# Weight sums made ahead in device memory for the paired down-projections of a two-block kernel

## The chip, the core and the metric

The kernel runs on one core of a Trainium2 chip. The time is the device time of one execution in microseconds (us), and less is better. The engines in the text: TensorE (PE), VectorE (DVE), ScalarE (ACT), GpSimd (POOL) and SyncE (SP), which here issues the loads of the weights. TensorE's granted clock was at its full level of 2.4 GHz (1.00) in all stretches read here.

## The reference

Two transformer blocks work on 256 rows of 2048 float32 values. The first has attention with compressed, selected and windowed keys (16 heads), a feed-forward of 8192 and a gated projection; the second has sliding-window attention with sinks (32 heads) and a gated feed-forward of 5632 with a short convolution. What matters here are the two down-projections:

```
h = h + y
hn = rms_norm(h, norm_ffn[i])
h = h + jnp.square(jax.nn.relu(hn @ ffn_w1[i])) @ ffn_w2[i]
...
c = conv_w[0] * up[:, 0:S]
for j in range(1, CONV_WIDTH_2):
    c = c + conv_w[j] * up[:, j:j + S]
gate, val = jnp.split(c, 2, axis=-1)
return (jax.nn.silu(gate) * val) @ w_down
```

## The kernel before

**Pieces.** All weights lie in device memory as `wstream`, 757 pieces of 128 x 1024 float32 (512 KB), in the order of use. SP loads one after another into the four slots of `raw` (L557), each as soon as the slot's old piece has its low half (`lo_ready`). ScalarE rounds a piece to its high half `whi` (`split_hi`, L2157), VectorE subtracts that from `raw` for the low half `wlo` (`split_lo`, L1307), and TensorE uses both: a product is three matmuls, high by high, high by low, low by high (`product`, L941 to L943). When TensorE has used a piece it raises `piece_used`, and the halves' slot is free.

**Stages.** Each takes a run of pieces: vs (first piece 0), kv (8), cv (40), misc (56), q (57), wo (89), then ff0, fd0, ff1, fd1, ff2, fd2, proj, ff3, fd3, gate, v2, k2, q2, wo2, and up0, dn0, up1, dn1, up2, dn2. A chunk of 2048 hidden columns is made in an ff or up stage and multiplied down in the fd or dn stage that follows. Every engine runs the same list of pieces by a loop of its own (`body` and `rows_body`), which splits a piece ahead and calls the steps that are due at an index (`between`), so the order of each engine's work is written out by hand. A wait in such a list holds up all that stands behind it on that engine.

**Paired stages.** fd0, fd1, fd2, dn0 and dn1 treat some pairs of pieces as a group (`Pairing`, `down_pair`). A plain pair needs 24 matmuls of 128 x 512: two pieces, two halves of columns, two halves of tokens, three each. A group gets the same from seven products of sums of weights and sums of hidden tiles, so 21. `FIRST` has groups at pairs 3 and 5 of both halves `cp` of the output columns (four a stage, three stages), `SECOND` at 4 and 6 of the first half and 2, 4 and 6 of the second (five a stage, two stages). The four products with sums of weights go to banks of their own (`side_bank`, ONE, FIVE, SEVEN, SIX) or to a main bank.

The weight sums are made in the stage: VectorE (in dn0 and dn1 POOL, but for the first group) adds halves of the two raw pieces (`t_first`: L1777 and L1779, on POOL L2736 and L2738), VectorE adds twice more (`t_second`: L1785, L1787), ScalarE rounds the four sums (`t_highs`, L2418, L2420) and VectorE subtracts for the low halves (`t_lows`, L1794):

```
V.tensor_tensor(sums_at(c)[:, 0, :], raw[:, x % SLOTS, 0:WIDE], raw[:, x % SLOTS, WIDE:], ALU.add)
V.tensor_tensor(sums_at(c)[:, 1, :], raw[:, x % SLOTS, WIDE:], raw[:, y % SLOTS, WIDE:], ALU.add)
V.tensor_tensor(sums_at(c)[:, 2, :], sums_at(c)[:, 0, :], y[:, WIDE:], ALU.add)
V.tensor_tensor(sums_at(c)[:, 3, :], sums_at(c)[:, 2, :], y[:, 0:WIDE], ALU.add)
```

At the end of a half's last group VectorE takes the side banks into the result (`sides_in`, five operations, L1807 to L1819, after ScalarE's `copy_side`), later the main banks (`mains_in`); TensorE's second half waits for the first of these. The sums of hidden tiles (`mix`, `mix_high`, `mix_low`) and the corrections (`corners`) are POOL's and ScalarE's.

**Around it.** In ff0 to ff3 ScalarE applies the rectifier and the square (`relu_squared`, L2373) one piece after TensorE has finished a tile, to `zr`, which POOL has made (`take`, L2661). In the q and q2 stages POOL scales the attention's probabilities (`nsa_scale`, L2691, and `swa_scale`) for TensorE's turns (L753 in q). ScalarE issues the load of `xrows` (2 MiB) in kv and six moves of V at the start of q (L2329 to L2338). POOL issues no transfer.

Of the kernel before, what the change touches and what calls it, by code (L numbers as in the profile page):

```python
# [26 lines left out]
P = 128  # L27
S = 256
# [36 lines left out]

STAGES = [("vs", 2, 16), ("kv", 16, 16), ("cv", 4, 32), ("misc", 3, 2), ("q", 16, 16), ("wo", 8, 16)]
# [12 lines left out]
_p = _u = _z = 0  # L79
for _name, _n, _k in STAGES:  # L80
    PB[_name], UB[_name], ZB[_name] = _p, _u, _z
# [95 lines left out]
class Pairing:  # L177


    def __init__(self, fast, sides, mains, last_sides):  # L180
        self.fast, self.sides, self.mains, self.last_sides = fast, sides, mains, last_sides
        self.mixed = sorted({m for ms in fast for m in ms})
        self.groups = [(cp, n, m) for cp, ms in enumerate(fast) for n, m in enumerate(ms)]
        self.x_at = {16 * cp + 2 * m: g for g, (cp, n, m) in enumerate(self.groups)}
        self.at_x = {g: x for x, g in self.x_at.items()}

    def used(self, cp):
        return len(self.fast[0]) + (len(self.fast[1]) if cp else 0)


FIRST = Pairing(((3, 5), (3, 5)), sides=12, mains=17, last_sides=28)
SECOND = Pairing(((4, 6), (2, 4, 6)), sides=14, mains=16, last_sides=32)
DN = FF_CHUNKS - 1


# [32 lines left out]
def program(nc, xT, pT, wstream, consts, setup, params, grows, xrows, out):  # L228
# [9 lines left out]
    bias_rows = nc.dram_tensor("bias_rows", [SWA_HEADS, RB], F32)  # L238

    with ExitStack() as ctx:  # L240
# [15 lines left out]
        with nc.sbuf_tensor("Tboth", [P, 2, 4, WIDE], FR) as Tboth:  # L256
            pass
        y = sb("y", [P, DT, S])

        with nc.sbuf_tensor("Tlow", [P, 4, WIDE], FR) as Tlow:  # L260
            pass
# [33 lines left out]
        def ring(flat, a, n=4, w=S):  # L295
# [4 lines left out]
        Tsum = ptf.rearrange("p (n c) -> p n c", n=4)  # L300
        Tcopy = [Tboth[:, h, :, :] for h in range(2)]
        tCf = tC.rearrange("p n w -> p (n w)")
        corner, cross = tCf[:, 0:WIDE], tCf[:, WIDE:2 * WIDE]
        mixsum = kT[:, :, :, :].rearrange("p a g c -> p (a g c)")[:, 0:3 * WIDE].rearrange("p (n i q) -> p n i q", n=3, i=4)
        mixed = [vT[:, 0:3, :].rearrange("p n (i q) -> p n i q", i=4),
                 mixlo[:, 4 * S:4 * S + 3 * WIDE].rearrange("p (n i q) -> p n i q", n=3, i=4)]
        Tsum2 = bflat[:, 4 * S:4 * S + 4 * WIDE].rearrange("p (n c) -> p n c", n=4)
        Tcopy2 = [vT[:, :, :], Tlow[:, :, :]]
        mixsum2 = bflat[:, 4 * S + WIDE:4 * S + 4 * WIDE].rearrange("p (n i q) -> p n i q", n=3, i=4)
        mixhi2 = mixhi[:, 0:3 * WIDE].rearrange("p (n i q) -> p n i q", n=3, i=4)  # L310
        mixlo2 = [pA[:, n, :, :].rearrange("p h (i q) -> p (h i) q", i=2) for n in range(2)]
        mixlo2.append(PTr.rearrange("p a b -> p (a b)")[:, 4 * (S + 4):4 * (S + 4) + 2 * S].rearrange("p (i q) -> p i q", i=4))
# [88 lines left out]
        t_sum, t_more, t_hi = Again(c_taken, 5 * KVG), Again(cpad_zero, 1), Again(c_exp, KVG)  # L401
        t_lo, t_used = Again(c_shift, KVG), Again(c_scores, KVG)
# [6 lines left out]
        x_scaled = sem("x_scaled")  # L409
# [29 lines left out]

        def sums_at(c):  # L440

            return Tsum2 if is_down2(c) else Tsum

        def sums_part(c, h):

            return (Tcopy2 if is_down2(c) else Tcopy)[h]
# [19 lines left out]
        def pairing(c):  # L466

            return SECOND if is_down2(c) else FIRST

# [73 lines left out]
        def _(sp):  # L543
# [11 lines left out]
            def load(i, s):  # L555
                sp.wait_ge(lo_ready, i - SLOTS + 1)
                sp.dma_start(raw[:, s, :], wstream[ds(i, 1)].rearrange("a p n -> p (a n)")).then_inc(raw_landed[s], 16)  # L557

            with sp.Fori(1, NPIECE // SLOTS - 1) as it:
                for j in range(SLOTS):  # L560
                    load(it * SLOTS + (SLOTS + j), j)
            for i in range(NPIECE // SLOTS * SLOTS, NPIECE):
                sp.wait_ge(lo_ready, i - SLOTS + 1)
                sp.dma_start(raw[:, i % SLOTS, :], wstream[i]).then_inc(raw_landed[i % SLOTS], 16)
            for t in range(QT):
                for f in range(4):

                    sp.wait_ge(fin_out, 4 * t + f + 1)
                    w = slice(f * WIDE, f * WIDE + WIDE)
                    sp.dma_start(out[:, t, w], xN[:, t, w]).then_inc(out_done, 16)  # L570
# [4 lines left out]
        def _(pe):  # L575
# [358 lines left out]
            def hidden(c, it, **more):  # L934
                ff, _, o = chunk_at(c)
                units(o * 64 + it * 8 + PB[ff], PB[ff], o * 24 + it * 4 + UB[ff], UB[ff], 4, DT,
# [8 lines left out]
            def down_pair(c, cp):  # L945

                _, fd, o = stage_at(c)
                p, z0 = o * 64 + (PB[fd] + 16 * cp), o * 24 + (4 + UB[fd])
                early, late = slice(0, P), slice(P, 2 * P)

                def weights(i, f):

                    s, w = (PB[fd] + 16 * cp + i) % SLOTS, slice(f * WIDE, f * WIDE + WIDE)
                    return whi[:, s, w], wlo[:, s, w]

                def hidden(i, tok):

                    return H[:, i, 0, tok], H[:, i, 1, tok]

                def mix_of(m, i):  # L960

                    return tuple(mixed_at(c, pairing(c).mixed.index(m), h)[:, i, :] for h in range(2))

                def sums(i):

                    return sums_part(c, 0)[:, i, :], sums_part(c, 1)[:, i, :]

                def arrive(i):

                    pe.wait_ge(lo_ready, p + (i + 1))  # L970
                    if cp == 0 and is_down2(c):
                        pe.wait_ge(up_ready, (c - DN) * CH + i + 1)
                    elif cp == 0:
                        pe.wait_ge(ff_ready, c * CH + (i + 1))

                def plain(i, f):

                    for t in range(QT):
                        last = product(main_bank(c, cp, 2 * f + t), *hidden(i, slice(t * P, t * P + P)), *weights(i, f), i == 0, i == 15)
                    return last  # L980

                def group(i, g):

                    _, n, m = pairing(c).groups[g]
                    lone, final = n == 0, n == len(pairing(c).fast[cp]) - 1
# [1958 lines left out]
```

## Time and profile before

| what | us |
|---|---|
| median of 3 runs | 2193.86 (2193.68 to 2193.93) |
| profiled execution, its own time | 2195.73 |
| its span | 2193.9 |
| TensorE busy | 2180.1 (99%) |
| VectorE busy | 1566.5 (71%) |
| ScalarE busy | 1133.5 (52%) |
| POOL busy | 711.8 (32%) |

Busy shares are averages over stages with different limits. Matmuls are pipelined: the time of one in a row is longer than the distance between two starts. A timeline row gives the start, the duration, and in brackets how long the engine had been idle and what released it; "x3" joins three of the same kind. In a window row the counts in brackets are instructions; then come TensorE's granted clock, the busy share of the 16 DMA engines and what they moved.

### The profile page before, as it was taken

Reading aid. Unit: us, or ns where it says so; the run is one execution under the profiler, and the core shown is the slowest. Engines: PE = TensorE matmul, PEld = TensorE weight load, DVE = VectorE, ACT = ScalarE, POOL = GpSimd, SP = SyncE. Lnnn points to the kernel's source line nnn. Section 1 sums busy time; section 2 is a strip of 40 time slices with the busy share of each in tenths; the row PEclk is TensorE's granted clock in tenths of the full one; section 3 lists DMA queues with packets and bytes.
Section 4 is the critical chain, followed back from the end, with each engine's and each line's share of the span. In section 5 each row is a group of like instructions: output and inputs, shape, how many; then the busy total and the mean of one; then the engine's idle time right before and its main releaser. Section 6 shows DMA issues by size and latency. Waiting matters only on the chain.

```text
span 2193.9 us, 34076 instructions
## 1 busy us (share of the span) xinstructions
PE 2180.1 (99%) x11511; PEld 1862.4 (85%) x11511; DVE 1566.5 (71%) x2187; ACT 1133.5 (52%) x1720; POOL 711.8 (32%) x625
## 2 busy tenths in 40 slices
PE   9999999999999999999999999999999999999998
PEld 7888988888888888888888887788888888888887
DVE  6876767558657757755878667567778777787775
ACT  6445555545445545454556455465455455554553
POOL 3202320361362263153000033005554355533531
PEclk9999999999999999999999999999999999999999
DMA  7665335556556556566565654545555665555664
GB/s 250 231 224 171 116 130 181 174 184 211 191 182 209 192 184 207 202 194 197 177 199 188 225 171 137 192 163 182 189 195 185 202 198 192 188 191 197 200 207 149
DMA packets 118084, 414.35 MB, mean 189 GB/s; under 512 B 12896, under 2 KB 18048, under 8 KB 117472
## 3 DMA queue, kind: packets, MB, share of 16 engines
q1 hardware_dynamic: 111600, 401.37, 55.7%
q10 hardware_dynamic: 6384, 11.70, 1.7%
q8 instruction: 57, 0.93, 0.2%
q14 instruction: 43, 0.35, 0.0%
HBM read 409.29 MB, written 2.15 MB: 188 GB/s over the span
## 4 chain that ended last, share of the span: by engine, by line
PE 93%; DVE 4%; ACT 1%; DMA 1%; POOL 1%; issue 1%; SPq 0%; DVEq 0%; ACTq 0%; POOLq 0%
PE bank L607 33%; PE bank L615 17%; PE bank L941 6%; PE bank L943 6%; PE bank L942 6%; PE bank L664 2%; PE bank L666 2%; PE bank L665 2%; DVE wboth L1307 2%; PE bank L1269 1%; PE bank L1267 1%; PE bank L1268 1%; PE bank L740 1%; PE bank L1202 1%; PE bank L777 1%; PE bank L917 1%
## 5 line engine op out<-in xcount | busy, mean ns | idle before, releaser
L1307 DVE TENSOR_TENSOR wboth<-raw,wboth 128x1024 fp32r<-128x1024 f32 (+1 forms) x756 | 953.8, 1267 | 468.1 <-ACT wboth L2157 459.8
L2157 ACT CAST wboth<-raw 128x1024 fp32r<-128x1024 f32 (+1 forms) x756 | 773.0, 1034 | 469.3 <-PE bank L943 123.3
L607 PE MATMUL bank<-A,wboth 128*128 128x512 f32 x2928 | 705.4, 392 | 0.5 <-DVE wboth L1307 0.3
L607 PEld LDWEIGHTS bank<-A,wboth 128*128 128x128 f32 x2928 | 536.8, 188 | 105.3 <-issue 1.3
L615 PEld LDWEIGHTS bank<-A,wboth 128*128 128x128 f32 x2928 | 376.7, 191 | 14.8
L615 PE MATMUL bank<-A,wboth 128*128 128x256 f32 x2928 | 384.0, 283 | 0.0
L941 PE MATMUL bank<-wboth,H 128*128 128x512 f32 x508 | 197.8, 389 | 1.2 <-DVE wboth L1307 1.2
L943 PE MATMUL bank<-wboth,H 128*128 128x512 f32 x508 | 197.6, 389 | 0.0
L942 PE MATMUL bank<-wboth,H 128*128 128x512 f32 x508 | 197.6, 389 | 0.0
L2661 POOL TENSOR_TENSOR PT<-z,rs 128x256 f32<-128x256 f32 x88 | 92.5, 1052 | 263.4 <-DVE z L1338 261.3
L2661 POOL TENSOR_TENSOR bias<-z,rs 128x256 f32<-128x256 f32 x64 | 104.7, 1635 | 197.9 <-DVE z L1338 109.4
L1338 DVE TENSOR_REDUCE z<-bank 128x256 f32<-128x512 f32 x172 | 117.6, 685 | 12.2 <-PE bank L607 12.1
L2373 ACT ACTIVATE Sm<-bias 128x256 f32<-128x256 f32 x64 | 26.7, 418 | 171.2 <-POOL bias L2661 171.2
L941 PEld LDWEIGHTS bank<-wboth,H 128*128 128x128 f32 x508 | 95.4, 188 | 21.8 <-DVE wboth L1307 2.0
L943 PEld LDWEIGHTS bank<-wboth,H 128*128 128x128 f32 x508 | 95.4, 188 | 19.8
L942 PEld LDWEIGHTS bank<-wboth,H 128*128 128x128 f32 x508 | 95.4, 188 | 19.7
L2766 POOL TENSOR_TENSOR x<-x,Sm 128x512 f32<-128x512 f32 x18 | 35.4, 1995 | 206.8 <-DVE x L1841 137.6
L2611 ACT ACTIVATE PT<-PT,par 128x256 f32<-128x256 f32 x88 | 44.8, 509 | 98.0 <-POOL PT L2661 98.0
L2661 POOL TENSOR_TENSOR kT<-z,rs 128x256 f32 (+1 forms) x12 | 11.3, 946 | 248.8 <-DVE z L1338 248.8
L2077 DVE SCALAR_TENSOR_TENSOR Sm<-PT,par 128x256 f32<-128x256 f32 x88 | 50.4, 573 | 51.7 <-ACT PT L2611 51.7
L2805 POOL TENSOR_TENSOR bias<-Sm 128x256 f32<-128x256 f32 x44 | 72.4, 1645 | 39.6 <-DVE Sm L2080 39.3
L607 PE MATMUL bank<-H,wboth 128*128 128x512 f32 x320 | 79.1, 394 | 0.0
(387 smaller groups left out, 3160.7 us busy)
## 6 DMA issues: line engine op xcount, KB each, us to landing
raw<-wstream SPq DMA_DIRECT2D x756, 512.0 KB, 3.4
bias<-bias_rows ACTq DMA_DIRECT2D x6, 512.0 KB, 5.4
x<-xrows ACTq DMA_DIRECT2D x1, 2048.0 KB, 9.1
bias<-grows ACTq DMA_DIRECT2D x2, 1024.0 KB, 6.4
out<-x SPq DMA_DIRECT2D x8, 256.0 KB, 2.1
x<-xT SPq DMA_DIRECT2D x7, 256.0 KB, 5.3
pA<-bias_rows ACTq DMA_DIRECT2D x2, 512.0 KB, 6.9
Sm<-grows ACTq DMA_DIRECT2D x1, 1024.0 KB, 6.6
```

The lines of the kernel that those rows point to most:

```text
L607: last = nc.tensor.matmul(bank(j)[:, :], whi[:, s, cols(i)], moving(j, k), start=(k == 0), stop=(k == K - 1))
L615: last = nc.tensor.matmul(bank(j)[:, 0:S], wlo[:, s, cols(i)], moving(j, k)[:, 0, :], start=False, stop=False)
L941: nc.tensor.matmul(bank[:, :], a_hi, w_hi, start=start, stop=False)
L942: nc.tensor.matmul(bank[:, :], a_hi, w_lo, start=False, stop=False)
L943: return nc.tensor.matmul(bank[:, :], a_lo, w_hi, start=False, stop=stop)
L1307: V.tensor_tensor(wlo[:, s, 0:w], raw[:, s, 0:w], whi[:, s, 0:w].bitcast(F32), ALU.subtract).then_inc(lo_ready, 1)
L1338: V.tensor_reduce(dst(j) if dst else z[:, (z0 + j) % 4, :], bank[:, :].rearrange("p (h c) -> p c h", h=2), AX, ALU.add).then_inc(z_ready, 1)
L2077: V.scalar_tensor_tensor(tA[:, slot, :], ub[:, slot, 1:S + 1], w[1], c0[:, slot % 2, :], ALU.mult, ALU.add).then_inc(up_step, 1)
L2157: C.copy(whi[:, s, 0:w], raw[:, s, 0:w]).then_inc(hi_ready, 1)
L2611: C.activation(c0[:, j % 2, :], ub[:, j % 4, 0:S], ACT.Copy, scale=par[:, ds(PO["conv"][0] + 3 * (2 * t0 + j), 1)]).then_inc(up_c0, 1)
L2661: return lambda zz: G.tensor_tensor(dst, zz, by, ALU.mult)
L2805: G.tensor_tensor(zr[:, slot + 1, :], tC[:, slot, :], tB[:, slot + 1, :], ALU.mult).then_inc(up_h, 1)
```

## The change

A tensor `weight_sums` in device memory takes, for each of now 24 groups, two pieces of 512 KB with the four sums.

- SP issues 24 plain copies of 1 MiB within device memory (both raw pieces of a group), twelve after the loads of pieces 11, 15, ... 55 (kv and cv), twelve from piece gate + 3 on, every fourth piece, which ends in v2.
- POOL issues transfers that add in device memory: for each group one of 512 KB and one of 256 KB (`sum_first`), then one of 512 KB (`sum_last`). Those of fd0 and fd1 and the first part of fd2's go out in q, fd2's last ones in wo; those of dn0 and dn1 in q2, dn1's last ones in wo2.
- In the paired stages a group is now four entries of the list: piece w + 1 (512 KB), the first half of piece w (256 KB), and the two pieces of sums (512 KB each, loaded by SP into `y` or `kT`, and then cast and subtracted like any piece: `sum_hi`, `sum_lo`). The order of products in a group is main 0, main 2, ONE, FIVE, SEVEN, SIX, main 1. `t_first`, `t_second`, `t_highs` and `t_lows` are gone on all engines.
- `SECOND` has six groups, at pairs 2, 4 and 6 of both halves. The mixed hidden tiles get other buffers. `sides_in` and `copy_side` stand four entries behind the beginning of a half's last group.
- ScalarE's `relu_squared` comes two pieces behind TensorE instead of one (`each_lag=2`).
- SP's and POOL's loops are written out with fixed addresses, and some semaphores are used again.

```diff
+FIRST = Pairing(((3, 5), (3, 5)))
+SECOND = Pairing(((2, 4, 6), (2, 4, 6)))
...
+            def load_pairs(c):
...
+                    if m in at.fast[cp]:
+                        g = at.used(0) * cp + at.fast[cp].index(m)
+                        load(PB[fd] + i, wstream[w + 1], past[0])
+                        load(PB[fd] + i + 1, wstream[w, :, 0:WIDE], past[1])
+                        if g == 0:
+                            sp.wait_ge(sums_done, 16 * group_of(c + 1, 0))
...
+                        for h in range(2):
+                            load_sum(c, i + 2 + h, g, h)
...
+            def sum_copy(c, g):
+
+                if c and g == 0:
+                    sp.wait_ge(sums_copied, 16 * group_of(c, 0))
+                x, n = first_weight(c, g), group_of(c, g)
+                sp.dma_start(weight_sums[2 * n:2 * n + 2], wstream[x:x + 2]).then_inc(sums_copied, 16)
...
+            copy_at = {**{PB["kv"] + 3 + 4 * i: at for i, at in enumerate(early)}, **{PB["gate"] + 3 + 4 * i: at for i, at in enumerate(late)}}
...
-                    product(side_bank(c, cp, ONE), *hidden(i, early), *weights(i, 0), lone, final).then_inc(piece_used, 1)
+                    arrive(i, 2 * m + 1)
+                    product(main_bank(c, cp, 0), *hidden(2 * m + 1, early), *weights(i, 0))
+                    pe.wait_ge(*mix_ready.at(mix_count(c, at.mixed.index(m) + 1)))
+                    product(main_bank(c, cp, 2), *mix_of(m, 3), *weights(i, 1)).then_inc(piece_used, 1)
                     arrive(i + 1)
-                    product(main_bank(c, cp, 0), *hidden(i + 1, early), *weights(i + 1, 0))
-                    pe.wait_ge(*mix_ready.at(mix_count(c, pairing(c).mixed.index(m) + 1)))
-                    product(main_bank(c, cp, 2), *mix_of(m, 3), *weights(i + 1, 1)).then_inc(piece_used, 1)
-                    pe.wait_ge(*t_lo.at(2 * group_of(c, g) + 1))
-                    product(side_bank(c, cp, FIVE), *mix_of(m, 1), *sums(0), lone, final)
-                    product(side_bank(c, cp, SEVEN), *mix_of(m, 0), *sums(1), lone, final)
-                    pe.wait_ge(*t_lo.at(2 * group_of(c, g) + 2))
-                    product(side_bank(c, cp, SIX), *mix_of(m, 2), *sums(2), lone, final)
-                    product(main_bank(c, cp, 1), *hidden(i + 1, late), *sums(3)).then_inc(t_used.sem, 1)
+                    product(side_bank(c, cp, ONE), *hidden(2 * m, early), *weights(i + 1, 0), lone, final).then_inc(piece_used, 1)
+                    arrive(i + 2)
+                    product(side_bank(c, cp, FIVE), *mix_of(m, 1), *weights(i + 2, 0), lone, final)
+                    product(side_bank(c, cp, SEVEN), *mix_of(m, 0), *weights(i + 2, 1), lone, final).then_inc(piece_used, 1)
+                    arrive(i + 3)
+                    product(side_bank(c, cp, SIX), *mix_of(m, 2), *weights(i + 3, 1), lone, final).then_inc(t_used.sem, 1)
+                    product(main_bank(c, cp, 1), *hidden(2 * m + 1, late), *weights(i + 3, 0)).then_inc(piece_used, 1)
...
-                steps_of.update({at.sides: lambda: sides_in(c, 0), at.mains: lambda: mains_in(c, 0, range(4)), at.last_sides: lambda: sides_in(c, 1),
-                                 30: lambda: mains_in(c, 1, range(2)), 31: lambda: mains_in(c, 1, range(2, 4))})
-                rows_body(p, PB[fd], 32, 1, lambda f: None, steps_of, 0, ahead, at.x_at)
+                steps_of = {at.over[0]: lambda: sides_in(c, 0), at.middle + (0 if is_down2(c) else 1): lambda: mains_in(c, 0, range(4)),
+                            at.count if is_down2(c) else at.over[1]: lambda: sides_in(c, 1),
+                            at.count - 2: lambda: mains_in(c, 1, range(2)), at.count - 1: lambda: mains_in(c, 1, range(2, 4))}
+                rows_body(o * CHP + PB[fd], PB[fd], at.count, 1, lambda f: None, steps_of, halves=at.halves, c=c)
...
-                body(o * 64 + it * 8 + PB[ff], PB[ff], o * 8 + it, 4, DT, relu_squared, **more)
+                body(o * CHP + it * 8 + PB[ff], PB[ff], it, 4, DT, relu_squared, each_lag=2, laps=o * CHUNK_LAPS, **more)
...
+            def sum_first(c, i):
+
+                g = i // 2
+                x, n = first_weight(c, g), group_of(c, g)
+                pool.wait_ge(sums_copied, 16 * group_of(c + 1, 0))
+                if i % 2:
+                    pool.dma_start(weight_sums[2 * n + 1, :, 0:WIDE], wstream[x + 1, :, WIDE:], accum_op=ALU.add).then_inc(sums_half, 16)
+                else:
+                    pool.dma_start(weight_sums[2 * n].rearrange("p (f w) -> p f w", f=2), wstream[x:x + 2, :, WIDE:].rearrange("a p w -> p a w"),
+                                   accum_op=ALU.add).then_inc(sums_half, 16)
...
+                pool.dma_start(weight_sums[2 * n + 1].rearrange("p (f w) -> p f w", f=2),
+                               weight_sums[2 * n, :, 0:WIDE].unsqueeze(1).to_broadcast([P, 2, WIDE]), accum_op=ALU.add).then_inc(sums_done, 16)
...
+                sums_early(i)
+            for g in range(len(FIRST.groups)):
+                pool.wait_ge(piece_used, SLOTS + PB["wo"] + 22 + 2 * g)
+                sum_last(2, g)
```

## Rows read from the trace of the kernel before

**Rows 1.** part 1 of the page: busy time of each engine, share of the span, instructions

```profile
PE 2180.1 (99%) x11511; PEld 1862.4 (85%) x11511; DVE 1566.5 (71%) x2187; ACT 1133.5 (52%) x1720; POOL 711.8 (32%) x625
```

**Rows 2.** waits of TensorE: line waited for, us in total, times, longest

```profile
PE bank L941 <- DVE wboth L1307: 1.2, 1, 1.2
```

**Rows 3.** windows: fd0, stretch of plain pieces; PE, PEld, DVE, ACT, POOL, clock, DMA, GB/s

```profile
520.30:531.18 10.88, 10.88 (x49) 9.01 (x49) 7.33 (x7) 4.21 (x4) 5.70 (x3) 1.00 0.67 230
```

**Rows 4.** timeline of TensorE in fd0 (start, us): the gap

```profile
501.39 0.39 PE L943 MATMUL bank<-wboth,H 128*128 128x512 f32 x1
502.95 0.50 PE L941 MATMUL bank<-wboth,H 128*128 128x512 f32 x1 [1.17 <-DVE wboth L1307]
```

**Rows 5.** timeline of VectorE at that gap

```profile
497.45 1.77 DVE L1777 TENSOR_TENSOR PT<-raw 128x512 f32<-128x512 f32 x1
...
501.06 0.69 DVE L1787 TENSOR_TENSOR PT<-PT,raw 128x512 f32<-128x512 f32 x1
501.67 1.22 DVE L1307 TENSOR_TENSOR wboth<-raw,wboth 128x1024 fp32r<-128x1024 f32 x1
```

**Rows 6.** all waits: ScalarE's before the rectifier

```profile
ACT Sm L2373 <- POOL bias L2661: 171.2, 64, 3.4
```

**Rows 7.** timeline of VectorE in dn0, sides at the turn

```profile
1678.24 0.69 DVE L1807 COPY y<-bank 128x512 f32<-128x512 f32 x1 [0.19 <-PE bank L943]
...
1680.76 0.69 DVE L1819 TENSOR_TENSOR Sm<-Sm,bank 128x512 f32<-128x512 f32 x1
```

**Rows 8.** timeline of TensorE there, first matmul after the group

```profile
1678.04 0.39 PE L941 MATMUL bank<-wboth,H 128*128 128x512 f32 x1
```

**Rows 9.** tile raw: durations min/median/max in ns of cast and subtract

```profile
L2157 ACT CAST wboth<-raw x756: 611/1048/1069, 9.5 to 2175.3; 128x1024 fp32r<-128x1024 f32 x179, 128x512 fp32r<-128x512 f32 x10
L1307 DVE TENSOR_TENSOR wboth<-raw,wboth x756: 676/1225/2596, 10.6 to 2176.4; 128x1024 fp32r<-128x1024 f32 x179, 128x512 fp32r<-128x512 f32 x10
```

**Rows 10.** windows: two of kv, two of cv, two of q, one of gate and v2

```profile
60.00:70.00 10.00, 10.00 (x57) 8.74 (x56) 7.88 (x11) 3.20 (x4) 0.74 (x1) 1.00 1.00 395
70.00:80.00 10.00, 10.00 (x57) 8.74 (x56) 8.89 (x9) 5.80 (x5) 3.12 (x2) 1.00 0.43 140
134.10:141.50 7.40, 7.40 (x41) 6.39 (x40) 3.93 (x5) 3.80 (x4) 0.00 (x0) 1.00 0.85 268
141.50:148.90 7.40, 7.40 (x41) 6.39 (x40) 4.90 (x4) 4.60 (x5) 0.00 (x0) 1.00 0.81 287
165.00:180.00 15.00, 15.00 (x83) 13.08 (x82) 8.68 (x16) 6.87 (x8) 2.21 (x3) 1.00 0.95 266
177.00:290.00 113.00, 113.00 (x709) 101.47 (x708) 82.57 (x242) 63.93 (x159) 34.22 (x37) 1.00 0.39 126
1080.00:1220.00 140.00, 139.76 (x633) 115.55 (x631) 112.28 (x176) 80.66 (x127) 0.00 (x0) 1.00 0.58 189
```

**Rows 11.** DMA issues: KB each, median us from issue to landing

```profile
x<-xrows ACTq DMA_DIRECT2D x1, 2048.0 KB, 9.1
```

**Rows 12.** timeline of TensorE in cv and at its end

```profile
137.81 1.11 PE L851 MATMUL bank<-wboth,H 128*120 128x256 f32 x8
...
145.21 1.11 PE L851 MATMUL bank<-wboth,H 128*120 128x256 f32 x8
...
152.97 0.42 PE L873 MATMUL bank<-A,wboth 128*48 128x512 f32 x1
```

**Rows 13.** timeline of VectorE in cv

```profile
131.75 2.36 DVE L1307 TENSOR_TENSOR wboth<-raw,wboth 128x1024 fp32r<-128x1024 f32 x2 [1.15 <-ACT wboth L2157]
...
141.94 3.73 DVE L1307 TENSOR_TENSOR wboth<-raw,wboth 128x1024 fp32r<-128x1024 f32 x3 [1.57 <-ACT wboth L2157]
...
148.95 2.52 DVE L1307 TENSOR_TENSOR wboth<-raw,wboth 128x1024 fp32r<-128x1024 f32 x2 [1.18 <-ACT wboth L2157]
```

**Rows 14.** timeline of POOL in q

```profile
186.42 2.96 POOL L2691 TENSOR_TENSOR Sm<-Sm,small 128x512 f32<-128x512 f32 x2
```

**Rows 15.** timeline of TensorE in q

```profile
191.43 0.82 PE L753 MATMUL bank<-con,Sm 128*128 128x128 f32 x6
```

More of the change, by code:

```diff
@@ L63, with __init__, used @@
 PW = BLK * P
+class Pairing:
+    def __init__(self, fast):
+        self.fast = fast
+        self.mixed = sorted({m for ms in fast for m in ms})
+        self.groups = [(cp, n, m) for cp, ms in enumerate(fast) for n, m in enumerate(ms)]
+        self.begin, at = {}, 0
+        for cp in range(2):
+            for m in range(8):
+                self.begin[cp, m] = at
+                at += 4 if m in fast[cp] else 2
+        self.middle, self.count = self.begin[1, 0], at
+        self.halves = {self.begin[cp, m] + 1 for cp, _, m in self.groups}
+        self.over = [self.begin[cp, fast[cp][-1]] + 4 for cp in range(2)]
+    def used(self, cp):
+        return len(self.fast[0]) + (len(self.fast[1]) if cp else 0)
+DN = FF_CHUNKS - 1
+FIRST = Pairing(((3, 5), (3, 5)))
+SECOND = Pairing(((2, 4, 6), (2, 4, 6)))
+PAIRED = {**{f"fd{c}": FIRST for c in range(DN)}, "dn0": SECOND, "dn1": SECOND}
+NGROUP = sum(len(at.groups) for at in PAIRED.values())
+CHP = 64 + 2 * len(FIRST.groups)
 STAGES = [("vs", 2, 16), ("kv", 16, 16), ("cv", 4, 32), ("misc", 3, 2), ("q", 16, 16), ("wo", 8, 16)]
@@ L553, in _, with load @@
             sp.dma_start(con[:, :], consts).then_inc(in_k, 16)
[L555 to L564, printed above, removed]
+            def load(i, src, past=SLOTS):
+                s = i % SLOTS
+                sp.wait_ge(lo_ready, i - past + 1)
+                sp.dma_start(raw[:, s, 0:src.shape[-1]], src).then_inc(raw_landed[s], 16)
@@ L960, in mix_of, with arrive @@
                 def mix_of(m, i):
[L962 to L968, printed above, removed]
+                    return tuple(mixed_at(c, at.mixed.index(m), h)[:, i, :] for h in range(2))
+                def arrive(i, k=None):
                     pe.wait_ge(lo_ready, p + (i + 1))
[L971 to L974, printed above, removed]
@@ L976, in plain @@
-                def plain(i, f):
+                    if cp == 0 and k is not None and is_down2(c):
+                        pe.wait_ge(up_ready, (c - DN) * CH + k + 1)
+                    elif cp == 0 and k is not None:
+                        pe.wait_ge(ff_ready, c * CH + (k + 1))
+                def plain(i, k, f):
                     for t in range(QT):
-                        last = product(main_bank(c, cp, 2 * f + t), *hidden(i, slice(t * P, t * P + P)), *weights(i, f), i == 0, i == 15)
+                        last = product(main_bank(c, cp, 2 * f + t), *hidden(k, slice(t * P, t * P + P)), *weights(i, f), k == 0, k == 15)
@@ L2128, in _ @@
                 if t == 0:
-                    dve.wait_ge(dn_half, 1)
+                    dve.wait_ge(*dn_half.at(1))
                 else:
@@ L2787, in _ @@
             pool.wait_ge(acc_zero, 1)
+            for g in range(len(SECOND.groups)):
+                pool.wait_ge(piece_used, SLOTS + PB["wo2"] + 16 + 2 * g)
+                sum_last(DN + 1, g)
             pool.wait_ge(rs_ready, 6)
```

322 lines of the change are left out of this document (166 added, 156 removed).

## The prediction

> **What bounds the kernel now.** I read the profile's first part, then TensorE's waits, and last the queues in the few places that the change touches. TensorE is busy for 2180.1 us, 99% of a span of 2193.9 us [rows 1]. Its waits are short and few; the one that this change can reach is a single 1.2 us at L941 for VectorE's L1307 [rows 2]. So time is won by fewer matmuls or by that wait, and lost wherever something new is late for TensorE. The pace is not the 389 ns of a row, which is a latency: in the paired stage fd0 49 matmuls start within 10.88 us [rows 3], and four plain pieces are 48, so one matmul of 128x512 costs 10.88/48 = 0.227 us.
>
> The sums below are made against the profiled execution, 2195.73 us, of which 2193.9 us are its span. The median of the runs is 2193.86 us, 1.87 us lower; I take the same difference off the median. 0.2% is 4.4 us, about what a measurement of this kernel can tell from no change: the lines lie at 2189.5 and 2198.2 us.
>
> **1. Fewer products.** The second pairing goes from five groups to six, in dn0 and in dn1. A group stands for a plain pair of pieces: 21 matmuls for 24. Two groups more are 6 matmuls: 6 x 0.227 = **-1.4 us**, all of it on TensorE's path.
>
> **2. The stall in fd0.** From the matmul at 501.39 to the next at 502.95 pass 1.56 us in place of 0.23 [rows 4]: 1.3 us lost; with a slow start behind it I take 1.4. VectorE explains it: between 497.45 and 501.75 it makes four additions of weights (L1777, L1779, L1785, L1787) with only one half-piece subtract among them, and the whole-piece subtract L1307 on which TensorE waits starts at 501.67 [rows 5]. All these additions leave the stage, so the subtract moves up by most of these 4.3 us; the copies now made for the sums are 3.5 pieces a group at 1.05 us on ScalarE and 1.22 us on VectorE [rows 9], 3.7 and 4.3 us against the group's 21 x 0.227 = 4.8 us of TensorE. Both fit. **-1.4 us.** No such wait stands in the other paired stages, so the additions taken out there give nothing; neither do the POOL additions of dn0 and dn1.
>
> **3. Rectifier and square a piece later.** ScalarE stood 171.2 us before L2373 for POOL, at most 3.4 us at a time [rows 6]. Behind that wait stand the casts of the next pieces. A piece later the wait is mostly over when it is asked for, and casts come earlier. TensorE, however, has no idle time in ff0 to ff2, so this is cover for step 2 and worth 0 itself. H is ready one piece later; the last tiles of H are read in the stage after, by its last pieces, and the first ones were made in the first quarter of the ff stage: 0.
>
> **4. The turn in dn0 and dn1 between the two halves of the columns.** Before, VectorE begins the five additions of the sides at 1678.24 us and ends at 1680.76 + 0.69 = 1681.45 [rows 7]. TensorE, from the matmul at 1678.04, has one plain pair to do before it needs those banks: 24 x 0.227 = 5.45 us, up to 1683.49 [rows 8]; 2.0 us were spare. After, the sides stand in the list behind the low half of the piece after next, whose slot the group's end frees: a cast of 1.05 and a subtract of 1.22 us [rows 9] go first. 2.3 + 3.2 = 5.5 us, with an assumed 0.15 us between the engines 5.65 us against 5.45: 0.2 us late, twice: **+0.4 us**. Both ends: 0 if the slot frees a product earlier, 1 us each if the cast waits behind another. In fd0 to fd2 two plain pairs, 10.9 us, lie there: nothing.
>
> **5. Copies in SP's queue.** SP issues 24 copies of 1 MiB from device memory to device memory among the loads of the weights, each in front of the next load. No row shows such a copy. Lower bound: the densest loads, 395 GB/s at a DMA share of 1.00 [rows 10], 1.049 MB in 2.65 us. Upper bound: read and written each at that price, 5.3 us. Between them lies the nearest row, the load of xrows: 2 MiB in 9.1 us from issue to landing, beside the weights' loads [rows 11], so 4.55 us a MiB. I take c = 4.5 us; both ends stay for the range.
>
> Where do they hurt? The twelve late ones fall in 1080 to 1220 us, where the engines are in use for 0.58 of the time [rows 10]; one copy comes with four pieces, and four pieces last 48 x 0.227 = 10.9 us, of which 0.42 x 10.9 = 4.6 us are free: c fits, 0. Eight early ones fall in kv: beside the load of xrows the share is 1.00, in the ten us behind it 0.43 [rows 10], so 10.9 us have some 6 us free for one copy: 0, with the copy beside xrows as the tightest. Four fall in cv, behind pieces 43, 47, 51 and 55. There four pieces go in 145.21 - 137.81 = 7.40 us [rows 12], which is 2.10 MB, 283 GB/s, and the DMA share is 0.85 and 0.81 [rows 10]: this stage is close to its loads. In such a cycle, which has one copy, the engines have 0.15 x 7.4 = 1.1 us free around copy 47 and 0.19 x 7.4 = 1.4 us around 51 and, I assume, 55. Then there is the lead of the low half over TensorE: 131.75 + 2.36 = 134.11 against 137.81, 3.7 us behind copy 47; 141.94 + 1.23 = 143.17 against 145.21, 2.0 us behind copy 51; 148.95 + 1.26 = 150.2 against 152.97, 2.8 us behind copy 55 [rows 12, 13]. Copy 43 has no smaller lead than 47. Each stall is c less the free time less the lead: at c = 4.5, 0 + 1.1 + 0.3 = **+1.4 us**; at 2.65, 0; at 5.3, 0.5 + 1.9 + 1.1 = 3.5; at 7, 2.2 + 3.6 + 2.8 = 8.6.
>
> The Trainium skill (DMA: Bandwidth & Descriptors, section Latency and other measured facts) states 207 to 214 GB/s in each direction for copies between tensors of device memory; by it, as an estimate, c would be 5.0 us and the whole sum 1.2 us higher than mine. No row here shows it.
>
> **6. POOL's accumulating transfers.** POOL issues 36 in q and wo and 36 later, on a queue of its own, for 1.25 MiB a group. It issues none before. In q the DMA share is 0.39 [rows 10]. Two places can feel it: the moves of V among the same engines, with a share of 0.95 in 165 to 180 us [rows 10], and POOL's own scaling: L2691 ends at 189.38 us and TensorE's turn L753 reads it at 191.43 [rows 14, 15], 2.05 us later, so an issue of under 2 us between them costs nothing. Lower end 0, upper end some 3 us (one late turn a whole scaling, 2.96 us [rows 14]). I take **+0.5 us**, near the lower end, since 2 us is the smallest slack that I found. The Trainium skill (DMA: Bandwidth & Descriptors, section Issuing engines are not separate DMA queues) says that such transfers share the 16 engines with the loads whatever queue issues them; it speaks against the change in the way already priced here.
>
> **7. More to load in the paired stages.** A group loads 1.75 MiB instead of 1. In dn a group and its plain pair are 45 x 0.227 = 10.2 us for 2.75 MiB, 2.88 MB: 282 GB/s. That is cv's rate, which runs there without a stall, and 395 GB/s were reached elsewhere: 0, covered by 2.9 us of spare DMA time in each such period; without that cover the rival C.
>
> **Sum.** -1.4 - 1.4 + 0.4 + 1.4 + 0.5 = -0.5 us: 2195.2 for a profiled execution, **2193.4 us** for the median.
>
> **Rivals.**
> A, slower: the copies hold up the loads in cv. Mechanism as in 5, place 134 to 153 us, price 3c - 12.4 us once all three stalls are open. Without it the sum is -1.9 us, so it takes 6.3 us of stall, c above 6.2 us (under 170 GB/s), to be slower by 0.2%; at c = 7 the time is 2193.86 - 1.9 + 8.6 = 2200.6 us. For it: the share of 0.81 to 0.85, and that a copy reads and writes the same memory. Against it: the upper bound from rows, 5.3 us, lies below 6.2, unless a copy's write is dearer than its read. Chance 0.22.
> B, all hidden: c near 2.65 us, and nothing from POOL. -1.4 - 1.4 + 0.4 = -2.4: 2191.5 us, still within 0.2%. For it: copies of large rows are the densest form of transfer, and TensorE stands nowhere in cv now. Chance 0.27.
> C, the sums arrive late: loads in dn fall to the 268 GB/s of cv's thinner stretch [rows 10], 2.88 MB in 10.75 us in place of 10.2, 12 periods: +6.5 us, 2199.7 us. Against it: cv's rate is what its pieces asked for. Chance 0.04.
> D, faster by over 0.2%: it would take 1.6 us more than steps 1 and 2 and no cost at all; no row offers that. Also, the change might not do what it says (sums that are waited for in full): that is C. Chance 0.05.
>
> **Numbers.** My forecast itself has 0.42 (c from about 3.5 to 6). Faster 0.05 (D), same 0.69 (forecast and B), slower 0.26 (A and C). The range reaches from B with step 4 at its lower end, 2191.0, to A at c = 7, 2200.6; outside are D, the far end of A and part of C, under 0.2.
>
> **What would show it.** TensorE's matmuls fall by 6; the interval of 1.56 us at fd0's first group is gone; in cv TensorE has one or two gaps of about a microsecond, released by the subtract to the low half, behind a wait of ScalarE for a load; the DMA share there nears 1; a gap of 0.2 us at the turns of dn0 and dn1. Wrong if: TensorE stands still in q or q2 behind POOL; if gaps appear inside groups (late sums); or if cv's gaps add up to more than 6 us.

## The result and the profile after

The changed kernel takes 2203.05 us (median of 5 runs, 2200.2 to 2205.89) against 2193.86 us (5 runs, 2193.45 to 2194.59): 9.2 us slower, ratio 1.0043 with a 95% interval of 1.0031 to 1.0054. That is above the range of the prediction. The times also scatter over 5.7 us, where those of the kernel before lie within 1.1 us (3.6 us over the 28 runs of a later set). The profiled execution of the changed kernel took 2201.86 us, with a span of 2200.0 us.

The page of the changed kernel: TensorE's busy time and instructions, then two DMA queues (packets, MB, share of 16 engines).

```profile
PE 2180.7 (99%) x11505; PEld 1863.1 (85%) x11505; DVE 1548.6 (70%) x2119; ACT 1146.8 (52%) x1724; POOL 731.9 (33%) x681
...
q1 hardware_dynamic: 119280, 445.41, 59.0%
q0 software_dynamic: 16512, 31.46, 8.5%
```

The six matmuls are gone (11505 in place of 11511 [rows 1]), and still the span is longer. q0 is new: POOL's adding transfers. They hold the engines for 0.085 x 2200 = 187 us for 31.46 MB, 168 GB/s. The loads and SP's plain copies, in q1, move 445.41 MB in 0.590 x 2200 = 1298 us, 343 GB/s. By the time of its packets, a byte added takes twice as long as a byte of q1.

TensorE's waits in the changed kernel (line waited for, us, times, longest), the three longest:

```profile
PE bank L817 <- POOL y L2706: 3.3, 1, 3.3
PE bank L854 <- DVE PTr L1590: 2.1, 1, 2.1
PE bank L938 <- DVE bias L1701: 2.1, 1, 2.1
```

The wait of [rows 2] is not among them; these three are new. Where they lie is told best by the same matmul, counted from the first, in the two timelines:

| place | before, us | after, us | after less before | lost here |
|---|---|---|---|---|
| start of kv | 44.29 | 41.93 | -2.4 | |
| end of cv | 152.60 | 152.75 | 0.15 | 2.5 |
| q, behind the first long wait | 189.81 | 196.45 | 6.6 | 6.5 |
| q, behind the second | 280.14 | 289.14 | 9.0 | 2.4 |
| fd0, first group | 502.95 | 510.41 | 7.5 | -1.5 |
| first matmuls ahead of up0 | 1458.77 | 1465.76 | 7.0 | -0.5: 0.2 close behind the row above, 0.3 here |
| dn0, the turn | 1683.03 | 1690.34 | 7.3 | 0.3 |
| dn2 | 2185.70 | 2191.79 | 6.1 | -1.2: six matmuls -1.4, dn1's turn 0.3 |

The first line is no work of the change: the first 44 us differ from the kernel before by -2.4 to 1.2 us in the profiled executions below, and between kernels that do the same there (1.2 in five, -2.1 in seven). From there on the change lost 8.5 us net: 11.4 us in cv and q and 0.6 at the turns, against some 3.4 us won.

**The wait of 3.3 us at 187 us.** The DMA issues (KB each, median us from issue to landing) of the changed kernel:

```profile
weight_sums<-wstream POOLq DMA_DIRECT2D x24, 512.0 KB, 9.4
weight_sums<-weight_sums POOLq DMA_DIRECT2D x24, 512.0 KB, 8.9
...
H<-H ACTq DMA_DIRECT2D x1, 256.0 KB, 13.2
vT<-PT ACTq DMA_DIRECT2D x1, 256.0 KB, 6.2
H<-PT ACTq DMA_DIRECT2D x1, 256.0 KB, 9.7
```

The same two moves of `H` in the DMA issues of the kernel before:

```profile
H<-H ACTq DMA_DIRECT2D x1, 256.0 KB, 6.9
H<-PT ACTq DMA_DIRECT2D x1, 256.0 KB, 6.6
```

Then ScalarE's timeline there in the changed kernel, and a row of POOL's with two of TensorE's; the brackets give the idle time ahead.

```profile
174.62 1.05 ACT L2202 CAST wboth<-raw 128x1024 fp32r<-128x1024 f32 x1 [1.72 <-PE bank L692]
182.84 0.47 ACTq L2392 DMA_DIRECT2D vT<-PT  x1
...
184.06 1.05 ACT L2202 CAST wboth<-raw 128x1024 fp32r<-128x1024 f32 x1 [8.40 <-issue]
...
193.05 1.99 ACT L2202 CAST wboth<-raw 128x1024 fp32r<-128x1024 f32 x2 [5.02 <-DMA H<-PT]
```

```profile
189.97 0.72 POOL L2706 TENSOR_TENSOR y<-z,bias 128x256 f32<-128x256 f32 x1 [9.26 <-DVE z L1782]
...
186.33 1.11 PE L692 MATMUL bank<-A,wboth 128*128 128x256 f32 x8
190.74 1.22 PE L817 MATMUL bank<-kT,y 128*128 128x256 f32 x2 [3.30 <-POOL y L2706]
```

The two last moves of `H` landed 13.2 and 9.7 us after issue, in place of 6.9 and 6.6 us. ScalarE waits for the first before it issues the next pair, and for the second before it goes on: the first is issued at 169.59 and lands 13.2 us later, at 182.8, where the next issue stands. So it stood 8.4 us and then 5.0, and its casts stand behind those waits. VectorE's subtract, its reduction for `y`, POOL's scaling of `y` and TensorE's scores follow in a chain; POOL had been idle for 9.26 us when the reduction released it. And the wait has a sequel. Windows of the changed kernel (columns as in [rows 3]):

```profile
190.00:195.00 5.00, 4.26 (x12) 3.54 (x13) 1.58 (x2) 1.95 (x2) 4.55 (x5) 0.50 1.06 304
195.00:200.00 5.00, 5.00 (x27) 4.38 (x27) 4.17 (x13) 3.08 (x12) 0.88 (x2) 0.84 1.00 233
```

TensorE's granted clock is 0.50, 1.2 GHz in place of 2.4, for the matmuls behind the wait; the mean of 0.84 in the second window puts its end at 196.6 us, 5.9 us behind the wait's end. Counted matmul by matmul, of the 6.5 us 0.2 lie ahead of the wait, 3.5 are the wait and 2.8 the slow matmuls.

**The wait of 2.1 us at 287 us.** POOL, VectorE, ScalarE and TensorE in their timelines of the changed kernel:

```profile
279.92 1.04 POOL L2756 DMA_DIRECT2D weight_sums<-weight_sums  x1 [6.92 <-DMA weight_sums<-weight_sums]
280.50 2.52 POOL L2736 TENSOR_TENSOR Sm<-Sm,small 128x512 f32<-128x512 f32 x2
...
280.59 2.47 DVE L1573 TENSOR_SCALAR small<-small 128x8 f32<-128x8 f32 x1
...
283.09 0.40 ACT L2278 ACTIVATE Sm<-Sm,small 128x128 f32<-128x128 f32 x1 [3.88 <-DVE small L1573]
...
289.14 0.50 PE L854 MATMUL bank<-PTr,vT 128*128 128x256 f32 x2 [2.10 <-DVE PTr L1590]
```

POOL stood 6.92 us in its list for a transfer that it had issued itself at 271.93: the first last addition of fd1 waits until those of fd0 have landed. The scaling queued behind, L2736, was so late that it began 0.09 us ahead of VectorE's L1573. That operation on 8 columns, 0.17 us in the kernel before (L1493 at 273.86), took 2.47 us and ended with POOL's. ScalarE's exponentials, VectorE's `PTr` and TensorE came 2 us later. The Trainium skill (SBUF — State Buffer, section Who interferes with whom) says that VectorE, in the two-port modes that an operation of this kind can enter, and GpSimd share a port pair, which the one that issues first holds for its whole instruction while the other stands. That VectorE stood for POOL this trace bears out: the two ends, 280.59 + 2.47 and 280.50 + 2.52, agree within 0.04 us. It stood for two instructions of POOL (x2), though, and who was first does not decide it in run one below.

**The wait of 2.1 us at the end of cv.** ScalarE, VectorE and TensorE in their timelines of the changed kernel:

```profile
150.06 1.05 ACT L2202 CAST wboth<-raw 128x1024 fp32r<-128x1024 f32 x1 [1.27 <-DMA raw<-wstream]
...
151.14 1.23 DVE L1381 TENSOR_TENSOR wboth<-raw,wboth 128x1024 fp32r<-128x1024 f32 x1 [1.09 <-ACT wboth L2202]
152.28 0.42 DVE L1701 TENSOR_REDUCE bias<-bank 120x128 f32<-120x256 f32 x1
...
150.28 0.39 PE L799 MATMUL bank<-wboth,A 128*128 128x512 f32 x1
152.75 0.66 PE L938 MATMUL bank<-con,bias 120*128 120x60 f32 x4 [2.08 <-DVE bias L1701]
```

This is the chain of step 5: a load behind a copy, a cast, a subtract. TensorE does not wait for the subtract itself but for the reduction that stands behind it in VectorE's list. In the kernel before, this reduction ended 0.8 us ahead of the matmul that needs it:

```profile
151.39 0.42 DVE L1621 TENSOR_REDUCE bias<-bank 120x128 f32<-120x256 f32 x1
...
152.60 0.55 PE L861 MATMUL bank<-con,bias 120*128 120x60 f32 x4
```

### The profile page after: what moved, and what is told of

It is laid out like the page before. It is cut to its first block, busy times and chain, and to the rows that moved or that the text cites. A ratio compares the mean times of both kernels' runs of the same rounds, so it can differ in the third digit from the quotient of the medians.

```text
span 2200.0 us, 31525 instructions
## 1 busy us (share of the span) xinstructions
PE 2180.7 (99%) x11505; PEld 1863.1 (85%) x11505; DVE 1548.6 (70%) x2119; ACT 1146.8 (52%) x1724; POOL 731.9 (33%) x681
## 3 DMA queue, kind: packets, MB, share of 16 engines
q1 hardware_dynamic: 119280, 445.41, 59.0%
q0 software_dynamic: 16512, 31.46, 8.5%
## 4 chain that ended last, share of the span: by engine, by line
PE 92%; DVE 5%; ACT 1%; DMA 1%; issue 1%; DVEq 0%; POOL 0%; ACTq 0%
PE bank L684 33%; PE bank L692 17%; PE bank L1018 6%; PE bank L1019 6%; PE bank L1020 6%; PE bank L741 2%; PE bank L743 2%; PE bank L742 2%; DVE wboth L1381 2%; PE bank L817 1%; PE bank L1341 1%; PE bank L1342 1%; PE bank L1343 1%; DMA raw<-wstream 1%; PE bank L854 1%; PE bank L1276 1%
## 5 line engine op out<-in xcount | busy, mean ns | idle before, releaser
L1381 DVE TENSOR_TENSOR wboth<-raw,wboth 128x1024 fp32r<-128x1024 f32 x756 | 962.0, 1283 | 382.6 <-ACT wboth L2202 378.0
L2202 ACT CAST wboth<-raw 128x1024 fp32r<-128x1024 f32 x756 | 778.9, 1035 | 588.5 <-PE bank L692 162.4
L1018 PE MATMUL bank<-wboth,H 128*128 128x512 f32 x520 | 202.7, 390 | 0.3
L1019 PE MATMUL bank<-wboth,H 128*128 128x512 f32 x520 | 202.5, 389 | 0.0
L1020 PE MATMUL bank<-wboth,H 128*128 128x512 f32 x520 | 202.5, 389 | 0.0
L2795 POOL TENSOR_TENSOR Sm<-Sm 128x256 f32<-128x256 f32 x64 | 81.1, 1267 | 136.0 <-ACT Sm L2428 136.0
L1018 PEld LDWEIGHTS bank<-wboth,H 128*128 128x128 f32 x520 | 97.6, 188 | 21.4 <-DVE Sm L1864 1.1
L1020 PEld LDWEIGHTS bank<-wboth,H 128*128 128x128 f32 x520 | 97.7, 188 | 20.3
L1019 PEld LDWEIGHTS bank<-wboth,H 128*128 128x128 f32 x520 | 97.6, 188 | 20.1
L2706 POOL TENSOR_TENSOR kT<-z,rs 128x256 f32 (+1 forms) x12 | 12.3, 1029 | 246.1 <-DVE z L1412 246.1
L741 PE MATMUL bank<-wboth,H 128*128 128x512 f32 x192 | 75.0, 390 | 0.0
```

The lines of the kernel that those rows point to most:

```text
L741: nc.tensor.matmul(bank[:, :], src[:, k, 0, tok], whi[:, s, w], start=(k == 0), stop=False)
L1018: nc.tensor.matmul(bank[:, :], a_hi, w_hi, start=start, stop=False)
L1019: nc.tensor.matmul(bank[:, :], a_hi, w_lo, start=False, stop=False)
L1020: return nc.tensor.matmul(bank[:, :], a_lo, w_hi, start=False, stop=stop)
L1381: V.tensor_tensor(wlo[:, s, 0:w], raw[:, s, 0:w], whi[:, s, 0:w].bitcast(F32), ALU.subtract).then_inc(lo_ready, 1)
L2202: C.copy(whi[:, s, 0:w], raw[:, s, 0:w]).then_inc(hi_ready, 1)
```

## Experiments

The theory after the comparison: the adding transfers of POOL take DMA time from the moves of V (`vT` and `H` in the rows above), POOL's wait for its own transfers costs the second stall, and the copies cost the one in cv. The rivals stand in the expectations.

**One: the first adding transfers behind the moves of V.**

```diff
-                if 1 <= i < 4 * n + 1:
-                    sum_first(*divmod(i - 1, 2 * n))
+                if 2 * n + 1 <= i < 4 * n + 1:
+                    for j in range(2):
+                        sum_first(*divmod(2 * (i - 2 * n - 1) + j, 2 * n))
```

> The first sixteen adding transfers of q (fd0 and fd1) go out at pieces 9 to 16 of q, two a piece, instead of one at each of pieces 1 to 16: none while the moves of V are under way. Theory T (the adding transfers share the DMA engines with the moves of V, ScalarE stands for these moves, 8.4 and 5.0 us in the changed kernel, and the chain over VectorE and POOL reaches TensorE at 187 us): the 6.5 us lost between 187 and 195 us go, down to 0 to 1; the stall at 287 us stays; about 2196.5 us in place of 2203.0. Rival R1 (it is the loads of weights, catching up after the copies in cv, that slow the moves): nothing changes in q, 2203. Rival R2 (POOL's time for the issues, 1.0 to 1.3 us each, makes its own work late): with two issues a piece the stalls grow, over 2203.

Measured: 2196.02 us (2194.12 before in the same set). The DMA issues of this kernel:

```profile
H<-H ACTq DMA_DIRECT2D x1, 256.0 KB, 6.2
vT<-PT ACTq DMA_DIRECT2D x1, 256.0 KB, 4.1
H<-PT ACTq DMA_DIRECT2D x1, 256.0 KB, 6.1
```

The moves land as before the change, and the first wait is gone, with the copies in cv still there: R1 falls. R2 falls too, since POOL now issues two transfers a piece and no new stall comes, and since in the changed kernel POOL stood idle for VectorE at this place. The Trainium skill (DMA: Bandwidth & Descriptors, section Issuing engines are not separate DMA queues) has the rule of step 6, that transfers share the 16 engines whatever queue issues them; that ScalarE's moves land in 6.2 and 6.1 us once POOL's transfers are out of their way, in place of 13.2 and 9.7, agrees with it.

The second stall stays, 2.2 us of waiting. VectorE and POOL here:

```profile
275.07 2.71 DVE L1573 TENSOR_SCALAR small<-small 128x8 f32<-128x8 f32 x1
...
275.21 2.52 POOL L2736 TENSOR_TENSOR Sm<-Sm,small 128x512 f32<-128x512 f32 x2
```

VectorE's operation begins 0.14 us ahead of POOL's scaling (0.32 us ahead in run three) and still ends with it. POOL's issue of a transfer, from 274.64, was under way by then. What held VectorE from its start, the issue or the scaling, no run shows.

This wait also has a sequel that the changed kernel's has not. The window behind it, and the one behind the equally long wait (2.2 us) of run three:

```profile
283.80:287.10 3.30, 3.25 (x15) 3.23 (x16) 2.61 (x5) 0.99 (x2) 2.31 (x3) 0.50 1.09 179
```

```profile
289.80:293.10 3.30, 3.30 (x25) 3.17 (x26) 2.71 (x6) 1.71 (x3) 2.38 (x3) 1.00 1.07 166
```

In one the granted clock was 0.50 and the stall cost 1.5 us more; in three it was 1.00. What decides it, the runs do not show.

**Two: fd1's last additions in wo.**

```diff
-                elif 5 * n + 2 <= i < 7 * n + 2:
+                elif 5 * n + 2 <= i < 6 * n + 2:
...
-            for g in range(len(FIRST.groups)):
-                pool.wait_ge(piece_used, SLOTS + PB["wo"] + 22 + 2 * g)
-                sum_last(2, g)
+            for c, first in ((1, 6), (2, 22)):
+                for g in range(len(FIRST.groups)):
+                    pool.wait_ge(piece_used, SLOTS + PB["wo"] + first + 2 * g)
+                    sum_last(c, g)
```

> The last four adding transfers of fd1 go out in wo instead of at pieces 26 to 29 of q, so that POOL does not wait in q for those of fd0 to land (6.9 us at 273 us). Theory T: POOL's scaling is then not late, it does not fall on VectorE's small operation (2.47 us in place of 0.17), and the 2.4 us at 287 us go: about 2200.6 us in place of 2203.0; the stall at 187 us stays. A rival, that the operation of VectorE and with it the stall come from the DMA traffic of these transfers as such: the traffic of fd0's four stays, so 1 us or more of the stall stays, 2202 or more.

Measured: 2199.42 us. VectorE and POOL in this kernel's timelines:

```profile
279.88 0.17 DVE L1573 TENSOR_SCALAR small<-small 128x8 f32<-128x8 f32 x1
...
274.74 2.04 POOL L2736 TENSOR_TENSOR Sm<-Sm,small 128x512 f32<-128x512 f32 x2 [2.44 <-DVE small L1582]
```

POOL's scaling is five us ahead of VectorE's operation, which takes 0.17 us again, and TensorE's wait at L854 is gone, so the rival falls; the stall at 187 us stays. In the three profiles in which POOL's wait makes the scaling fall on this operation (the changed kernel, this run's neighbours one and three) it took 2.47, 2.71 and 2.88 us.

**Three: fd2's copies in q.**

```diff
-            copy_at = {**{PB["kv"] + 3 + 4 * i: at for i, at in enumerate(early)}, ...
+            copy_at = {**{PB["kv"] + 3 + 4 * i if i < 8 else PB["q"] + 17 + 4 * (i - 8): at for i, at in enumerate(early)}, ...
```

> The four copies of 1 MiB for fd2 go out behind pieces 17, 21, 25 and 29 of q instead of behind four pieces of cv. Theory T: the gaps of 0.3 and 2.2 us in cv go, the 6.5 us at 187 us stay: about 2200.5 us in place of 2203.0. Rival R1: without the copies nothing has to catch up at the beginning of q, the moves of V land in time and both stalls go, 2194.

Measured: 2200.29 us. TensorE's longest waits in this kernel:

```profile
PE bank L817 <- POOL y L2706: 4.7, 1, 4.7
PE bank L854 <- DVE PTr L1590: 2.2, 1, 2.2
```

The wait at L938 is gone and both in q stay, the first with 7.6 us lost in place of 6.5: R1 falls a second time.

**Four: no adding transfers.** The diff takes out the three transfers of POOL with their waits; SP waits for the copies in place of the sums.

> No adding transfers at all, so the paired stages multiply with the raw copies in place of the sums; the plain copies and all else stay. Theory T: both stalls in q go (6.5 and 2.4 us), the one in cv (2.5 us) and those of the turns (0.4 us twice) stay: 2194 us. Rival R1: only the 2.4 us at 287 us go, 2200.6. Rival R2 gives 2194 like T; the first run of this set tells those two apart.

Measured: 2194.20 us, 8.9 us under the changed kernel, whose median is from another set (the kernel before: 2193.86 there, 2194.12 here). Both stalls of q are gone from TensorE's waits, the one in cv is 1.5 us in this profile. So the adding transfers, beside the moves of V and by POOL's wait for them, are the whole of what was lost in q.

**Five and six: everything moved, with and without an earlier turn.** Five has the three diffs above and this one; six has only the three.

```diff
-                steps_of = {at.over[0]: lambda: sides_in(c, 0), ...
+                steps_of = {at.over[0] - (1 if is_down2(c) else 0): lambda: sides_in(c, 0), ...
...
-                steps_of.update({at.over[0]: lambda: copy_side(c, 0), ...
+                steps_of.update({at.over[0] - (1 if is_down2(c) else 0): lambda: copy_side(c, 0), ...
```

> The three moves of the first set together (adding transfers behind the moves of V, fd1's last ones in wo, fd2's copies in q), and in dn0 and dn1 the sides are taken in one entry earlier at the turn, ahead of the low half that waits for the group's end. Theory T: all that the change cost is gone (6.5, 2.4, 2.5 us and 0.4 us twice) and what it gained stays, 1.4 us for six matmuls and 1.5 us in fd0: about 2191 us, 2.9 us under the kernel before. Rival: moved transfers collide at their new places and take back what was won, 2194 us or more.

> As the run with all four, but the sides at the turn stay where the change put them. Theory T: 0.4 us more in each of dn0 and dn1, 0.8 us over that run, about 2192; in the trace two waits of 0.3 us at the turns, which the other has not. Rival: the cast that stands ahead is no matter, both kernels show the same waits and the same time.

Measured: 2190.99 and 2191.44 us, against 2194.64 us before in this set: ratios 0.9983 (0.9974 to 0.9992) and 0.9984 (0.9975 to 0.9993). Both beat both kernels. Between the two the difference of the medians, 0.45 us, is within the scatter; the traces tell them apart. TensorE's timeline at the turn of dn0 without the earlier sides, then with them:

```profile
1680.44 0.39 PE L1020 MATMUL bank<-wboth,H 128*128 128x512 f32 x1
1680.97 0.50 PE L1018 MATMUL bank<-wboth,H 128*128 128x512 f32 x1
```

```profile
1681.59 0.39 PE L1020 MATMUL bank<-wboth,H 128*128 128x512 f32 x1
1681.81 0.39 PE L1018 MATMUL bank<-wboth,H 128*128 128x512 f32 x1
```

0.53 us from start to start without, 0.22 with; the matmul behind the gap is slower too, by 0.1 us. dn1 shows the same. From 44 us to the last matmuls the kernel without takes 0.9 us longer.

**Seven and eight: what took the stall in fd0 away?** Seven sets `each_lag=1` in the kernel of five; eight is the kernel before with `each_lag=2` alone:

```diff
-                    for step, behind in ((late, lag), (each, 1)):
+                    for step, behind in ((late, lag), (each, each_lag)):
...
-                body(o * 64 + it * 8 + PB[ff], PB[ff], o * 8 + it, 4, DT, relu_squared, **more)
+                body(o * 64 + it * 8 + PB[ff], PB[ff], o * 8 + it, 4, DT, relu_squared, each_lag=2, **more)
```

> As the run with all four, but ScalarE's rectifier and square stand one piece behind TensorE again, as before the change. Theory T: the stall in fd0 went because VectorE's additions left the stage, so it stays away: the same time, about 2191. Rival: it went because ScalarE's casts no longer wait for POOL; then 1.2 to 1.5 us come back at fd0's first group, about 2192.4.

> The kernel before, with only ScalarE's rectifier and square a piece later in ff0 to ff3. Theory T: VectorE's four additions still stand ahead of the subtract that TensorE waits for, so the wait in fd0 stays, 0.8 us or more of 1.5: 2193 to 2194. Rival: with earlier casts VectorE comes to its additions earlier and the wait goes: about 2192.5.

Measured: 2190.81 us for seven, the same as five. For eight 2192.94 us, 1.7 us under the kernel before in its set, but with an interval that reaches no change (ratio 0.9991, 0.9981 to 1.0); the trace decides, and my theory fell there. VectorE's timeline of eight:

```profile
491.90 1.77 DVE L1777 TENSOR_TENSOR PT<-raw 128x512 f32<-128x512 f32 x1
...
496.12 1.22 DVE L1307 TENSOR_TENSOR wboth<-raw,wboth 128x1024 fp32r<-128x1024 f32 x1
```

The same additions stand ahead of the same subtract and take the same time, but all of it is 5.5 us earlier than in [rows 5], and the first matmul of that piece starts at 500.12 with no wait. In seven, too, TensorE's matmuls at fd0's first group follow each other in 0.23 us. Either edit alone takes the whole stall away; the two together win it once.

**Nine: plain copies in place of the adding ones.** The diff takes `accum_op=ALU.add` from POOL's three transfers.

> The changed kernel with POOL's transfers as plain copies of the same bytes at the same places; nothing is added, so the paired stages multiply with copied weights in place of sums. In the changed kernel the adding transfers take 8.5% of 16 engines' span for 31.46 MB, 187 us, 168 GB/s; the weights' loads run at 343 GB/s by the same reckoning. If the adding makes them dear (the destination must be read too), the plain ones take about half, the moves of V land up to 4 us sooner and the 6.5 us at 187 us shrink to 3 or less: 2199 or less. If it is the bytes, or the queue of POOL, the share stays at 8 to 9% and the time at 2203.

Measured: 2198.97 us. From the page, the DMA issues and VectorE's timeline of this kernel:

```profile
q0 software_dynamic: 8832, 31.46, 4.2%
...
H<-H ACTq DMA_DIRECT2D x1, 256.0 KB, 12.3
...
H<-PT ACTq DMA_DIRECT2D x1, 256.0 KB, 7.6
...
277.54 1.52 DVE L1609 TENSOR_TENSOR bias<-bias 128x128 f32<-128x128 f32 x1
```

The share halves, 4.2% or 92 us for the same bytes, so the adding itself is what makes them dear. The packets halve with it, from 16512 to 8832, at about the same time each (187 x 16 / 16512 = 0.18 us, 92 x 16 / 8832 = 0.17): the trace shows twice the packets, and not that reading the destination is what costs. But the first move of `H` still takes 12.3 us (13.2 with the adding, 6.9 before the change), the second 7.6, and the stall at 187 us shrinks only from 6.5 to 4.5 us, not to 3 as expected: extra transfers at that place are enough for most of it, and half their DMA time gave back little of the first move's delay. The stall at 287 us goes from 2.4 to 1.2 us: POOL's wait is 4.6 in place of 6.9 us, so its scaling falls on another operation of VectorE, L1609, which takes 1.52 us in place of 0.29 (in the changed kernel), while L1573 takes 0.17 again.

**Ten: five groups in the second pairing.** In the kernel of five, `SECOND = Pairing(((4, 6), (2, 4, 6)))`.

> As the run with all four, but the second pairing with five groups as before the change: six matmuls of 128x512 more. Theory T: 6 times 0.227 us, 1.4 us over that run, about 2192.4 us, with no wait of TensorE added or removed. Rival: a sixth group costs in DMA or in VectorE what it saves in TensorE; the same time as that run, 2191.

Measured: 2191.82 us, 0.8 us over five in the medians, and 1.6 if each is taken against the kernel before in its own set (2193.91 here, 2194.64 there). In the timelines, from 44 us to the last matmuls, this kernel is 2.5 us under the kernel before and five is 3.9: 1.4 us for six matmuls, as the pace says. The sixth group costs nothing that the traces show.

## Why the prediction was wrong, point by point

- **Step 6 failed; it carries the miss.** It took 0.5 us with 3 at the most, and the runs show 8.9 (four). Its first place was right, the moves of V at a DMA share of 0.95, but I priced only POOL's issues and the scaling, never the DMA time of what POOL issues. The six transfers out by 180 us are 2.36 MB; even at the loads' rate they needed 7 us of engines that had 0.05 x 15 = 0.75 us free [rows 10], and at 168 GB/s it is 14 us. The bound of 3 us had no ground: behind ScalarE's waits stand the casts of the next pieces, and I did not follow them. The sequel, matmuls at half clock, was in no term. Bytes and DMA time do not give the size of the stall either: in nine half the DMA time left 4.5 of the 6.5 us. Why the moves are that much later is open.
- **A wait that I did not list.** POOL's wait for its own last additions stands in the diff; what was queued behind it on POOL, the scaling, I did not name. It cost 2.4 us, by way of a collision with VectorE that the lateness made, and 1.2 us in nine by a collision of the same kind. The prediction's own sign of being wrong, TensorE standing still in q behind POOL, came up at 187 us and, by way of VectorE, at 287.
- **Step 5 was right in stage and kind, and its size partly by luck:** 1.4 us taken, 2.4 to 2.5 us in the profiles of the changed kernel and nine, 1.5 in those of one, two and four. Inside the stage the sizes came out the other way round: 0.3 us where it had 1.1, 2.2 where it had 0.3. The lead of 2.8 us at the end of cv was counted to the matmul at 152.97; the one that waits, at 152.60, needs the reduction, which had a lead of 0.8. By its own formula the total is a copy of 4.5 to 4.95 us a MiB, between my 4.5 and the 5.0 worked out from the Trainium skill (DMA: Bandwidth & Descriptors, section Latency and other measured facts); with those leads wrong that is no measurement of a copy. Rival A, which had this place and a slower kernel, has the sign but not the cause: it needed over 6.2 us a copy. Kv and the late copies cost nothing, as said.
- **Step 4:** right in place, low in size: 0.4 us in each turn in place of 0.2. In dn0 four subtracts in a row, 4.63 us, stood ahead of the sides in VectorE's list, not one.
- **Steps 1 and 2:** right in size, 1.4 and 1.5 us, and shown by ten and by the wait that is gone.
- **Step 3 failed in its reason:** I gave the later rectifier no worth of its own. Alone it takes the stall away (eight); beside step 2 it has nothing left to win (seven).
- **Step 7:** right. No wait inside a group, so rival C fell.
- Some 0.3 us won ahead of up0 were not foreseen: TensorE's matmul there starts 0.23 us behind the one ahead in place of 0.50. Eight, with the later rectifier alone, does not have it (0.49); the cause stays open.

The kernel of five is the version to keep: 3.65 us under the kernel before in its set.

## What to carry to other kernels

Work that is moved off the engines into transfers is paid in DMA time: price every transfer by bytes and kind against the free share at the very place where it is issued, and follow what waits for the other transfers that are under way there. Such a price is a warning and no forecast, as nine shows. A wait that an engine makes for its own transfer belongs behind the work that others need from it. With two edits that could each remove the same stall, count it once.

## What the runs showed of the hardware

An adding transfer within device memory held the DMA engines twice as long for a byte as a plain one from the same queue (187 and 92 us for 31.46 MB), in twice as many packets. Beside such transfers a move of 256 KB landed in 13.2 us in place of 6.9, and in 12.3 beside plain ones of the same bytes. A wait of TensorE of 3.3 us was followed by 5.9 us at a granted clock of 0.50, which cost nearly as much again; of two waits of 2.2 us, one was followed by 3.3 us at 0.50 and one was not. An operation of VectorE on 8 columns took 2.5 to 2.9 us in place of 0.17 when POOL's issue and scaling fell on it, and ended with the scaling.
